# Five output projections whose two activation parts lie side by side and are read by one matmul of 512 columns

## The chip, the cores and the metric

One core of a Trainium2 chip runs the whole program as one launch. The metric is device time in microseconds, from the start to the end of one execution; lower is better. TensorE multiplies, ScalarE and VectorE convert, split and combine, GpSimd adds squares, and SyncE issues the DMAs that bring the weights.

## The reference

An activation `x` of 256 tokens by 1024 channels passes through two blocks. In the first, two layers each have a mixer (pooling with attention in layer 0, a gated recurrence in layer 1) and a convolutional feed-forward part of width 2816. The second has a mixer of four branches and a squared-ReLU feed-forward part of width 4096. Each part ends in a projection whose result is added to `x`:

```python
x = x + (concat(pool, attention) @ pa_w_out)        # 1024 -> 1024
x = x + (conv_ffn_hidden @ ffn_w_out[0])            # 2816 -> 1024
x = x + (gelu(gate) * hs) @ rg_w_out                # 1280 -> 1024
x = x + (conv_ffn_hidden @ ffn_w_out[1])            # 2816 -> 1024
x = x + gt1 * (merged @ w_o)                        # 1024 -> 1024
x = x + gt2 * (square(relu(h @ ffn_w1)) @ ffn_w2)   # 4096 -> 1024
```

RMS norms stand between the parts, so each part needs the whole of `x` from the one before it. All inputs are 32-bit floats.

## The kernel before

Everything is held transposed: 128 channels on the partitions, 256 tokens (`T`) along the free dimension. A weight matrix comes in chunks of up to eight tiles of 128x128 by SyncE's DMAs into a ring of six buffers (`ring`, `NR`). Each chunk is split in two: ScalarE rounds it to the 32-bit replicated format (`whi`, printed fp32r in the rows), and VectorE subtracts that from the chunk to get the rest (`wlo`); there are five such pairs (`NS`). The functions called `feed` do this on both engines, three to four chunks ahead of the one that TensorE uses. Activations are split in the same way, into high and low parts (`hh`/`hl`, `hidh`/`hidl`, `pah`/`pal`, `mgh`/`mgl`).

A product is then three matmuls of 256 columns for each tile of 128 input channels, all added in one PSUM bank: high weights by high activation, high weights by low activation, low weights by high activation (`linear`, L488 to L502). I call these three a tile step. Each matmul is preceded by its own weight load.

The function `residual` makes one output tile `m` of 128 channels after another (for 1024 inputs the first two together). On TensorE it calls `linear`. On VectorE it first splits the chunks up to three ahead (`feed`, L1633), then waits for output tile `m` and adds it to `x` (`add_to_x`, L1619 to L1624; for the last two projections with a multiplication by a column of `mod`), then does extra work handed in as `also`, then makes the low part of the unscaled next activation (`low_of_h`). ScalarE squares each `x` tile, GpSimd adds the squares.

Behind each projection but the last, `early` (L504 on) lets TensorE begin three output tiles of the next part with the activation that is not yet normalised, its sums of squares after the second tile step (`stats`), while VectorE and ScalarE make the normalising row (`rst`), and then the scaled activation (`raw`, then `hh` and `hl`), which the next part waits for. In the `also` slot VectorE prepares parameters of later parts (`s5p`, `w`, `tmp`, `cf` in the rows). Each engine works strictly through its own order; semaphores stand between them.

Of the kernel before, what the change touches and what calls it, by code (L numbers as in the profile page):

```python
# [7 lines left out]
F32R = mybir.dt.float32r  # L8
# [4 lines left out]
T = 256  # L13
# [207 lines left out]
def build(nc, d, out):  # L221
    with ExitStack() as ctx:
        cnt = [0]

        def alloc(stack, name, shape, dt=F32):
            cnt[0] += 1
            return stack.enter_context(nc.sbuf_tensor(f"{name}_{cnt[0]}", shape, dt))

        def signal(name):
# [32 lines left out]
        sq = alloc(st, "sq", [128, 4, T])  # L262
        vf = alloc(st, "vf", [128, 4, T])
        vt = alloc(st, "vt", [128, 2, 512])
        pah = alloc(st, "pah", [128, 8, T], F32R)
        pal = alloc(st, "pal", [128, 8, T], F32R)
        ta = alloc(st, "ta", [128, 16 + T])
        tb = alloc(st, "tb", [128, 16 + T])
        pw = alloc(st, "pw", [128, 4, 128])
# [8 lines left out]
        st.close()  # L278

        st = ExitStack()  # L280
        hidh = [alloc(st, "hidh", [128, 22, T], F32R)] * 2
        hidl = [alloc(st, "hidl", [128, 22, T], F32R)] * 2
        zu = [alloc(st, "zu", [128, 3, T])] * 2
        zg = [alloc(st, "zg", [128, 3, T])] * 2
        zl = [alloc(st, "zl", [128, 3, T])] * 2
# [14 lines left out]
        st.close()  # L300

        st = ExitStack()
        hidh[1] = alloc(st, "hidh", [128, 22, T], F32R)
        hidl[1] = alloc(st, "hidl", [128, 22, T], F32R)
        zu[1] = alloc(st, "zu", [128, 3, T])
        zg[1] = alloc(st, "zg", [128, 3, T])
        zl[1] = alloc(st, "zl", [128, 3, T])
# [25 lines left out]
        ws = alloc(s2, "ws", [128, 4, 128])  # L333
        bs_ = alloc(s2, "bs", [128, 4, 128])
        gvT = alloc(s2, "gvT", [128, 2, 256])
        mgh = alloc(s2, "mgh", [128, 8, T], F32R)
        mgl = alloc(s2, "mgl", [128, 8, T], F32R)
        bd = alloc(s2, "bd", [128, 2, 2, 64])
        cd = alloc(s2, "cd", [128, 2, 8, 16])
        cc = alloc(s2, "cc", [128, 2, 8, 16])  # L340
# [1 line left out]
        st.close()  # L342

        st = ExitStack()
        hid2h = alloc(st, "hidh2", [128, 32, T], F32R)
        hid2l = alloc(st, "hidl2", [128, 32, T], F32R)
        zz = alloc(st, "zz", [128, 4, T])
        st.close()

        MR = [mrow[:, :].rearrange("p (h t) -> p h t", h=4),  # L350
              sqt[:, 0:2, :].rearrange("p a t -> p (a t)").rearrange("p (h t) -> p h t", h=4)]

        def v4(a):
            return a[:, :, :].rearrange("p a t -> p (a t)").rearrange("p (z h t) -> p z h t", z=2, h=4)
# [82 lines left out]
        where = {}  # L437
# [23 lines left out]
        def tensor_program(e):  # L461
# [70 lines left out]
                mm(p[:, 0:T], ones, sqt[:, 2, :], False).then_inc(*stat.up(n))  # L532
                give(("stat", n), mean, n)

            def residual(n, w, nk, of, need, also=None):
                for ms in ([0, 1], [2], [3], [4], [5], [6], [7]) if nk == 8 else [[m] for m in range(8)]:
                    linear(w, ms, of, nk, need)
                    for m in ms:
                        give((w, m), resid, (n, m))
                        if also:  # L540
                            also(m)
# [32 lines left out]
            def pool_attn():  # L574
# [101 lines left out]
                    if m == 0:  # L676
                        mod_step()

                residual(1, "pa_w_out", 8, pair(pah, pal), lambda k: at_dve.wait_ge(e, ("pal", k)), also)

            def conv_ffn(l):
                w = f"ffn_w_in{l}"
                n = 2 * l + 1
                early(n)
                for i, at in enumerate(EARLY[n]):
                    give(at, ff_dve, (l, "lift", i))
                project(w, [23, 2], n)
                give((w, 23), ff_dve, (l, "g", 1))
                give((w, 2), ff_dve, (l, "u", 2))
                for m in range(2, 22):  # L690
                    if m > 2:
                        project(w, [m], n)
                        give((w, m), ff_dve, (l, "u", m))
                    project(w, [m + 22], n)
                    give((w, m + 22), ff_dve, (l, "g", m))
                    if m in ADA_IN[l]:
                        mod_step()

                def also(m):
                    mod_turn()  # L700

                residual(2 * l + 2, f"ffn_w_out{l}", 22, pair(hidh[l], hidl[l]), lambda k: ff_dve.wait_ge(e, (l, "lo", k)), also)

            def rglru():
                def ri(m):
# [57 lines left out]
            def mixers():  # L763
# [231 lines left out]
                        next(steps[at])  # L995
                for m in range(8):
                    y_of(m, 0)
                residual(5, "w_o", 8, pair(mgh, mgl), lambda k: mx_dve.wait_ge(e, ("ml", k)))

            def relu_ffn():  # L1000
                early(5)
# [13 lines left out]
            conv_ffn(1)  # L1015
            mixers()
            relu_ffn()
            residual(6, "ffn_w2", 32, pair(hid2h, hid2l), lambda k: ff_dve.wait_ge(e, (2, "lo", k)))
            stats(6)


# [524 lines left out]
        def vector_program(e):  # L1546
# [69 lines left out]
                    e.tensor_copy(shw[:, i:i + 1], ps[where[w, m]][:, T:T + 1]).then_inc(*shifted.up((n, i)))  # L1616
                return tt(o, p, rst[:, :], MUL)

            def add_to_x(n, m, p):  # L1619
                if n < 5:  # L1620
                    tt(x[:, m, :], p, x[:, m, :], ADD).then_inc(*resid.up((n, m)))
                else:
                    g = 16 if n == 5 else 40
                    stt(x[:, m, :], p, mod[:, g + m:g + m + 1], x[:, m, :], MUL, ADD).then_inc(*resid.up((n, m)))  # L1624

            def add_squares(n, m):
                square.wait_ge(e, (n, m))
# [3 lines left out]
            def residual(n, w, nk, also=None):  # L1631
                for ms in ([0, 1], [2], [3], [4], [5], [6], [7]) if nk == 8 else [[m] for m in range(8)]:
                    feed(tail(w, ms[-1], nk))  # L1633
                    for m in ms:
                        add_to_x(n, m, out_of(w, m, nk))
                        if also:
                            also(m)
                        if m and n < 6:
                            low_of_h(n, m - 1)
                if n < 6:  # L1640
                    low_of_h(n, 7)
                    feed(first(n))
# [278 lines left out]
            def rglru():  # L1921
                stat.wait_ge(e, 2)

                def taps(m):
                    src = xl[:, m, :] if m < 3 else out_of("rg_w_in", m + 10)
                    rg_act.wait_ge(e, ("x", m))
                    for s in (1, 2, 3):
                        stt(xr[:, m, s:], src[:, 0:T - s], P("rg_cw", (3 - s) * 10 + m), xr[:, m, s:], MUL, ADD).then_inc(*rg_dve.up(("x", m, s)))
                        rg_dve.wait_ge(e)
                    rg_dve.alias(("x", m))  # L1930

                def sizes(ms):
                    for m in ms:
                        rg_act.wait_ge(e, ("square", m))
                        stt(xr[:, m, :], sc[:, m % 4, :], 1.0, xr[:, m, :], ADD, MUL).then_inc(*rg_dve.up(("size", m)))

                def scan(m):
                    rg_act.wait_ge(e, ("root", m))
                    rg_pool.wait_ge(e, ("ix", m))
                    tt(ii[:, m, :], ii[:, m, :], xr[:, m, :], MUL).then_inc(*rg_dve.up(("b", m)))  # L1940
                    rg_dve.wait_ge(e)
                    rg_act.wait_ge(e, ("decay", m))
                    e.tensor_tensor_scan(xr[:, m, :], rr[:, m, :], ii[:, m, :], 0.0, MUL, ADD).then_inc(*rg_dve.up(("scan", m)))

                def times_gate(m):
                    rg_act.wait_ge(e, ("gelu", m))
                    rg_dve.wait_ge(e)
                    tt(gate[:, m, :], gate[:, m, :], xr[:, m, :], MUL).then_inc(*rg_dve.up(("y", m)))

                def low_of_y(m):  # L1950
                    rg_act.wait_ge(e, ("yh", m))
                    low_of(yl[:, m, :], gate[:, m, :], yh[:, m, :]).then_inc(*rg_dve.up(("yl", m)))

                h_tiles(2)
                for m in range(3):
                    lift(xl[:, m, :], 2, m).then_inc(*rg_dve.up(("lift", m)))
                for m in range(3):
                    taps(m)
                for m in range(3, 10):
                    feed(tail("rg_w_in", m + 10))  # L1960
                    taps(m)
                    if m in ADA_RG[0]:
                        mod_step()
                for m in range(10):
                    feed(tail("rg_w_in", m))
                    mod_turn()
                    if m in ADA_RG[1]:
                        mod_step()
                    sizes({2: (0, 1), 3: (2, 3, 4), 4: (5, 6, 7), 5: (8, 9)}.get(m, ()))
                    for i in {6: (0, 1), 7: (2,), 8: (3,), 9: (4,)}.get(m, ()):  # L1970
                        scan(i)
                    if m > 7:
                        times_gate(m - 8)
                    if m == 9:
                        low_of_y(0)
                for k in range(10):
                    if k < 5:
                        scan(k + 5)
                    if k < 8:
                        times_gate(k + 2)  # L1980
                    if k < 9:
                        low_of_y(k + 1)
                    if k == 9:
                        for m in range(8):
                            rg_pe.wait_ge(e, ("out", m))
                            add_to_x(3, m, ps[where["rg_w_out", m]][:, 0:T])
                            if m:
                                low_of_h(3, m - 1)
                        low_of_h(3, 7)
                    feed(number["rg_w_out", 0, k])  # L1990
                feed(first(3))
# [498 lines left out]
```

## Time and profile before

| | |
|---|---|
| median of 3 runs | 1174.78 us (1174.45 to 1177.47) |
| the profiled execution | 1179.18 us |
| its span, first to last instruction | 1177.4 us |
| mean granted TensorE clock | 0.975 of full |
| matmuls, and as many weight loads | 8588 |

The profile comes from one execution of its own, so sums of its rows are set against its span of 1177.4 us; 1.8 us lie around the span. L467 is the helper that issues every matmul, L1034 that of ScalarE's activations, L1551 (tensor_tensor), L1554 and L1557 those of VectorE; a row is told apart by its tile names. In matmul rows the time of one is longer than its distance to the next, since matmuls are pipelined: the distance between starts is what counts. In names such as ps<-hidh,whi the buffer number is left out, and hidh stands for the hidden activation of both feed-forward forms.

### The profile page before, as it was taken

The numbers are of one execution on the slowest core, as the hardware profiler recorded it, in microseconds if no ns is written. First come the engines' busy times: TensorE is split into PE (matmuls) and PEld (weight loads), VectorE is DVE, ScalarE is ACT, GpSimd is POOL, SyncE is SP. The second block draws the span as 40 slices with busy tenths as digits, with TensorE's granted clock in tenths as the row PEclk, the third lists the DMA queues.
The fourth block names the chain that finished last, engine by engine and source line by source line (L and its number), as shares of the span: only waits on it lengthen the run. The fifth ranks groups of instructions, "written<-read, shape, count | busy, mean of one in ns | idle before, by whom it ended". The sixth has DMA issues, their size and how long they took to land.

```text
span 1177.4 us, 21014 instructions
## 1 busy us (share of the span) xinstructions
PE 1093.6 (93%) x8588; PEld 1039.9 (88%) x8588; DVE 837.4 (71%) x1444; ACT 641.6 (54%) x1098; POOL 67.5 (6%) x79
## 2 busy tenths in 40 slices
PE   6997999999979788999999989899999979999996
PEld 6875999999978688899999978799989979999996
DVE  6464998888894486887787778898875576655443
ACT  6544676665645965655555585322233457875441
POOL 2131100000002001000001000000000011000010
PEclk9998999999999988999999989999999989999999
DMA  9267465555555573565675642222324274656641
GB/s 335 70 210 280 154 186 191 180 166 194 160 195 173 213 252 106 179 237 194 249 252 179 206 143 69 81 88 92 106 97 155 80 252 132 201 184 191 196 143 36
DMA packets 59856, 200.41 MB, mean 170 GB/s; under 512 B 6768, under 2 KB 11504, under 8 KB 59632
## 3 DMA queue, kind: packets, MB, share of 16 engines
q1 hardware_dynamic: 58032, 194.54, 49.9%
q10 hardware_dynamic: 1728, 4.53, 1.1%
q8 instruction: 68, 1.11, 0.4%
q14 instruction: 28, 0.23, 0.1%
HBM read 197.99 MB, written 1.05 MB: 169 GB/s over the span
## 4 chain that ended last, share of the span: by engine, by line
PE 75%; DVE 14%; ACT 6%; DMA 2%; issue 1%; SPq 0%; ACTq 0%; DVEq 0%
PE ps L467 75%; DVE wlo L1551 4%; ACT whi L1034 2%; DVE rst L1580 1%; ACT L1034 1%; DVE raw L1551 1%; DMA ring<-ffn_w_out 1%; DVE raw L1557 1%; DMA ring<-pa_w_in 1%; DVE hl L1557 1%; DVE hl L1551 1%; ACT rr L1034 0%; DVE x L1551 0%; ACT xr L1034 0%; ACT raw L1034 0%
## 5 line engine op out<-in xcount | busy, mean ns | idle before, releaser
L467 PE MATMUL ps<-hh,whi 128*128 128x256 f32 (+1 forms) x1656 | 484.1, 292 | 40.3 <-DVE wlo L1551 38.4
L467 PE MATMUL ps<-hh,wlo 128*128 128x256 f32 (+1 forms) x1656 | 473.7, 286 | 0.0
L467 PE MATMUL ps<-hl,whi 128*128 128x256 f32 (+1 forms) x1656 | 472.1, 285 | 0.0
L1551 DVE TENSOR_TENSOR wlo<-ring,whi 128x1024 fp32r<-128x1024 f32 (+1 forms) x313 | 376.4, 1217 | 66.7 <-ACT whi L1034 65.8
L1034 ACT ACTIVATE whi<-ring 128x1024 fp32r<-128x1024 f32 (+1 forms) x313 | 323.0, 1040 | 102.6 <-PE ps L467 62.1
L467 PEld LDWEIGHTS ps<-hh,whi 128*128 128x128 f32 x1656 | 319.1, 193 | 61.8 <-issue 32.9
L467 PEld LDWEIGHTS ps<-hl,whi 128*128 128x128 f32 x1656 | 319.8, 193 | 1.4 <-issue 1.0
L467 PEld LDWEIGHTS ps<-hh,wlo 128*128 128x128 f32 x1656 | 319.4, 193 | 0.0
L467 PE MATMUL ps<-hidh,whi 128*128 128x256 f32 x608 | 172.3, 283 | 2.3 <-DVE wlo L1551 2.3
L467 PE MATMUL ps<-hidl,whi 128*128 128x256 f32 x608 | 172.0, 283 | 0.0
L467 PE MATMUL ps<-hidh,wlo 128*128 128x256 f32 x608 | 172.0, 283 | 0.0
L467 PEld LDWEIGHTS ps<-hidh,whi 128*128 128x128 f32 x608 | 116.7, 192 | 3.4 <-DVE wlo L1551 1.8
L467 PEld LDWEIGHTS ps<-hidl,whi 128*128 128x128 f32 x608 | 116.7, 192 | 0.0
L467 PEld LDWEIGHTS ps<-hidh,wlo 128*128 128x128 f32 x608 | 116.7, 192 | 0.0
L2330 POOL TENSOR_TENSOR sqa<-sqa,sqt 128x256 f32<-128x256 f32 x36 | 34.2, 951 | 963.9 <-ACT sqt L1034 963.9
L1557 DVE SCALAR_TENSOR_TENSOR zg<-ps,vec,zg 128x255 f32<-128x255 f32 x84 | 40.4, 481 | 24.8 <-ACT zg L1034 23.2
L1034 ACT ACTIVATE sqt<-x 128x256 f32<-128x256 f32 x49 | 20.1, 414 | 65.7 <-DVE x L1551 34.1
L1557 DVE SCALAR_TENSOR_TENSOR zu<-ps,vec,zu 128x255 f32<-128x255 f32 x80 | 38.5, 481 | 17.0 <-ACT zu L1034 14.5
L1034 ACT ACTIVATE zg<-ps,vec 128x256 f32<-128x256 f32 x42 | 23.6, 562 | 47.1 <-PE ps L467 47.1
L1034 ACT ACT_TABLE_LOAD x35 | 44.9, 1283 | 6.4 <-issue 4.2
L1034 ACT ACTIVATE zu<-ps,vec 128x256 f32<-128x256 f32 x40 | 22.5, 563 | 29.8 <-PE ps L467 23.6
L467 PE MATMUL ps<-yin,ring 128*128 128x256 f32 x160 | 38.6, 379 | 0.0
(360 smaller groups left out, 1348.9 us busy)
## 6 DMA issues: line engine op xcount, KB each, us to landing
ring<-ffn_w_in SPq DMA_DIRECT2D x88, 512.0 KB, 4.3
ring<-ffn_w SPq DMA_DIRECT2D x64, 512.0 KB, 4.4
ring<-w_in SPq DMA_DIRECT2D x51, 512.0 KB, 3.6
ring<-ada_w SPq DMA_DIRECT2D x48, 512.0 KB, 5.2
ring<-ffn_w_out SPq DMA_DIRECT2D x32, 448.0 KB, 4.5
ring<-rg_w_in SPq DMA_DIRECT2D x20, 512.0 KB, 4.3
ring<-pa_w_in SPq DMA_DIRECT2D x16, 512.0 KB, 6.6
ring<-ffn_w_out SPq DMA_DIRECT2D x16, 512.0 KB, 3.7
```

What stands on the lines that cost most here:

```text
L467: return e.matmul(o, l, r, start=start, stop=stop)
L1034: return e.activation(o, i, func, bias=bias, scale=scale, accum_out=acc)
L1551: return e.tensor_tensor(o, a, b, op)
L1557: return e.scalar_tensor_tensor(out=o, in0=a, scalar=s, in1=b, op0=op0, op1=op1)
L1580: e.reciprocal(rst[:, :], rst[:, :]).then_inc(*mean.up(("rst", n)))
L2330: e.tensor_tensor(sqa[:, :], sqa[:, :], sqt[:, m % 2, :], ADD).then_inc(*sum_g.up((n, m)))
```

## The change

The high and low part of an activation get one array in which tile k's 256 high columns are followed by its 256 low columns. In five of the six projections (all but rg_w_out) one matmul of 512 columns reads both against the high weights and fills a whole bank: columns 0 to 255 hold high by high, columns 256 to 511 high by low. The matmul with the low weights still has 256 columns and adds to the first half. VectorE adds both halves to `x`, one after the other, and the second waits for the first. The arrays take the same room as before. Cut to its core:

```diff
-        pah = alloc(st, "pah", [128, 8, T], F32R)
-        pal = alloc(st, "pal", [128, 8, T], F32R)
+        pa2 = alloc(st, "pa2", [128, 8, 2, T], F32R)
...
+        (pah, pal), (mgh, mgl), (hid2h, hid2l) = ((a[:, :, 0, :], a[:, :, 1, :]) for a in (pa2, mg2, hid2))
+        hidh, hidl = ([a[:, :, v, :] for a in hid] for v in range(2))
...
+            def wide(w, ms, both, nk, need):
+                outs = [take((w, m)) for m in ms]
+                for parts in zip(*(chunks(w, m, nk) for m in ms)):
+                    k, n = parts[0][1:]
+                    for q in range(n):
+                        need(k + q)
+                        for (c, _, _), o in zip(parts, outs):
+                            low.wait_ge(e, c)
+                            j = turn[c] % NS
+                            last = k + q == nk - 1
+                            if last:
+                                mm(o[:, 0:T], wlo[j][:, q, :], both[:, k + q, 0, :], False, False)
+                            t = mm(o[:, :], whi[j][:, q, :], both[:, k + q, :, :], k + q == 0, last)
+                            if not last:
+                                t = mm(o[:, 0:T], wlo[j][:, q, :], both[:, k + q, 0, :], False, False)
+                            if q == n - 1:
+                                t.then_inc(*through.up(c))
...
-            def residual(n, w, nk, of, need, also=None):
+            def residual(n, w, nk, both, need, also=None):
                 for ms in ([0, 1], [2], [3], [4], [5], [6], [7]) if nk == 8 else [[m] for m in range(8)]:
-                    linear(w, ms, of, nk, need)
+                    wide(w, ms, both, nk, need)
...
-            def add_to_x(n, m, p):
-                if n < 5:
-                    tt(x[:, m, :], p, x[:, m, :], ADD).then_inc(*resid.up((n, m)))
-                else:
-                    g = 16 if n == 5 else 40
-                    stt(x[:, m, :], p, mod[:, g + m:g + m + 1], x[:, m, :], MUL, ADD).then_inc(*resid.up((n, m)))
+            def add_to_x(n, m, parts):
+                for i, p in enumerate(parts):
+                    if i:
+                        resid.wait_ge(e)
+                    if n < 5:
+                        t = tt(x[:, m, :], p, x[:, m, :], ADD)
+                    else:
+                        g = 16 if n == 5 else 40
+                        t = stt(x[:, m, :], p, mod[:, g + m:g + m + 1], x[:, m, :], MUL, ADD)
+                    t.then_inc(*resid.up((n, m) if p is parts[-1] else (n, m, i)))
...
-                        add_to_x(n, m, out_of(w, m, nk))
+                        p = out_of(w, m, nk)
+                        add_to_x(n, m, (p, ps[where[w, m]][:, T:2 * T]))
```

## Rows read from the trace of the kernel before

**Rows 1.** The page: busy time of the engines, share of the span, instructions.
```profile
PE 1093.6 (93%) x8588; PEld 1039.9 (88%) x8588; DVE 837.4 (71%) x1444; ACT 641.6 (54%) x1098; POOL 67.5 (6%) x79
```

**Rows 2.** The page: chain that ended last, shares of the span by engine.
```profile
PE 75%; DVE 14%; ACT 6%; DMA 2%; issue 1%; SPq 0%; ACTq 0%; DVEq 0%
```

**Rows 3.** Timeline in ffn_w2: start us, length us, engine, operation, tiles.
```profile
1163.05 0.28 PE L467 MATMUL ps<-hidl,whi 128*128 128x256 f32 x1
1163.05 0.19 PEld L467 LDWEIGHTS ps<-hidh,wlo 128*128 128x128 f32 x1
...
1166.05 0.28 PE L467 MATMUL ps<-hidh,wlo 128*128 128x256 f32 x1
```

**Rows 4.** Timeline of TensorE: matmuls of 258 columns behind w_o.
```profile
985.02 0.28 PE L467 MATMUL ps<-hh,whi 128*128 128x258 f32 x1
...
987.41 0.28 PE L467 MATMUL ps<-hh,wlo 128*128 128x258 f32 x1
```

**Rows 5.** Timeline of TensorE in pa_w_out, behind an idle stretch.
```profile
111.38 1.12 PE L570 MATMUL ps<-cst,mrow 128*128 128x128 f32 x4 [2.53 <-ACT mrow L1034]
...
112.94 0.41 PE L467 MATMUL ps<-pah,whi 128*128 128x256 f32 x1
...
114.22 0.41 PE L467 MATMUL ps<-pah,whi 128*128 128x256 f32 x1
```

**Rows 6.** Timeline of TensorE: matmuls in plain 32-bit, merged.
```profile
47.42 1.84 PE L467 MATMUL ps<-cst,sq 128*128 128x2 f32 x16
...
939.81 5.56 PE L467 MATMUL ps<-yin,ring 128*128 128x256 f32 x25
```

**Rows 7.** Chain of waits through pa_w_out and ffn_w_out0: start us, us, what.
```profile
116.42 0.42 DVE x L1551
...
131.80 0.35 DVE x L1551
...
142.31 157.45 PE ps L467 x1311
...
308.05 1.15 DVE wlo L1551
...
309.24 5.67 PE ps L467 x45
...
318.88 0.34 DVE x L1551
...
325.87 0.33 DVE x L1551
...
336.66 1.15 DVE wlo L1551
```

**Rows 8.** Chain of waits through ffn_w_out1.
```profile
602.28 8.15 PE ps L467 x66
...
610.87 55.45 PE ps L467 x462
...
666.34 0.42 DVE x L1551
```

**Rows 9.** Chain of waits through w_o.
```profile
953.28 27.95 PE ps L467 x211
...
981.26 0.44 DVE rst L1554
```

**Rows 10.** Chain of waits through ffn_w2 to the end.
```profile
1009.91 156.80 PE ps L467 x1308
...
1166.73 0.49 DVE x L1557
```

**Rows 11.** Timeline of VectorE around w_o, idle time before in brackets.
```profile
940.66 0.42 DVE L1551 TENSOR_TENSOR cosT<-ps,cosT 128x256 f32<-128x256 f32 x1 [1.81 <-PE ps L467]
941.12 0.42 DVE L1551 TENSOR_TENSOR cosT<-cosT,pm 128x256 f32<-128x256 f32 x1
...
978.22 0.48 DVE L1557 SCALAR_TENSOR_TENSOR x<-ps,mod,x 128x256 f32<-128x256 f32 x1 [0.70 <-PE ps L467]
...
979.99 1.22 DVE L1551 TENSOR_TENSOR wlo<-ring,whi 128x1024 fp32r<-128x1024 f32 x1
```

**Rows 12.** Windows: stretch, its us, VectorE busy us, clock, DMA share, GB/s.
```profile
602.00:666.00 64.00, 51.04 (x84) 1.00 0.63 208
```

More of the change, by code:

```diff
@@ L280, in build @@
         st = ExitStack()
-        hidh = [alloc(st, "hidh", [128, 22, T], F32R)] * 2
-        hidl = [alloc(st, "hidl", [128, 22, T], F32R)] * 2
+        hid = [alloc(st, "hid", [128, 22, 2, T], F32R)] * 2
         zu = [alloc(st, "zu", [128, 3, T])] * 2
@@ L302, in build @@
         st = ExitStack()
-        hidh[1] = alloc(st, "hidh", [128, 22, T], F32R)
-        hidl[1] = alloc(st, "hidl", [128, 22, T], F32R)
+        hid[1] = alloc(st, "hid", [128, 22, 2, T], F32R)
         zu[1] = alloc(st, "zu", [128, 3, T])
@@ L335, in build @@
         gvT = alloc(s2, "gvT", [128, 2, 256])
-        mgh = alloc(s2, "mgh", [128, 8, T], F32R)
-        mgl = alloc(s2, "mgl", [128, 8, T], F32R)
+        mg2 = alloc(s2, "mg2", [128, 8, 2, T], F32R)
         bd = alloc(s2, "bd", [128, 2, 2, 64])
@@ L344, in build @@
         st = ExitStack()
-        hid2h = alloc(st, "hidh2", [128, 32, T], F32R)
-        hid2l = alloc(st, "hidl2", [128, 32, T], F32R)
+        hid2 = alloc(st, "hid2", [128, 32, 2, T], F32R)
         zz = alloc(st, "zz", [128, 4, T])
@@ L677, in also @@
                         mod_step()
-                residual(1, "pa_w_out", 8, pair(pah, pal), lambda k: at_dve.wait_ge(e, ("pal", k)), also)
+                residual(1, "pa_w_out", 8, pa2, lambda k: at_dve.wait_ge(e, ("pal", k)), also)
             def conv_ffn(l):
@@ L700, in also @@
                     mod_turn()
-                residual(2 * l + 2, f"ffn_w_out{l}", 22, pair(hidh[l], hidl[l]), lambda k: ff_dve.wait_ge(e, (l, "lo", k)), also)
+                residual(2 * l + 2, f"ffn_w_out{l}", 22, hid[l], lambda k: ff_dve.wait_ge(e, (l, "lo", k)), also)
             def rglru():
@@ L997, in mixers @@
                     y_of(m, 0)
-                residual(5, "w_o", 8, pair(mgh, mgl), lambda k: mx_dve.wait_ge(e, ("ml", k)))
+                residual(5, "w_o", 8, mg2, lambda k: mx_dve.wait_ge(e, ("ml", k)))
             def relu_ffn():
@@ L1017, in tensor_program @@
             relu_ffn()
-            residual(6, "ffn_w2", 32, pair(hid2h, hid2l), lambda k: ff_dve.wait_ge(e, (2, "lo", k)))
+            residual(6, "ffn_w2", 32, hid2, lambda k: ff_dve.wait_ge(e, (2, "lo", k)))
             stats(6)
@@ L1985, in rglru @@
                             rg_pe.wait_ge(e, ("out", m))
-                            add_to_x(3, m, ps[where["rg_w_out", m]][:, 0:T])
+                            add_to_x(3, m, (ps[where["rg_w_out", m]][:, 0:T],))
                             if m:
```

## The prediction

> **What bounds the kernel now.** I read the page first: TensorE is busy 93% of the span and VectorE 71% [rows 1], and the chain that ended last is 75% TensorE and 14% VectorE [rows 2]. So a faster tile step on TensorE pays, but only where TensorE is on that chain, and 40 more VectorE operations cost wherever VectorE is. I therefore read the timeline for what one matmul takes from start to start, and then the chain of waits through each of the five projections.
>
> The slot. In ffn_w2 25 slots lie between the starts at 1163.05 and 1166.05 us, so one is 0.120 us, and the load of the next weights starts together with the matmul before it [rows 3]. A tile step is three slots, 0.360 us. What fills a slot decides everything, since the columns streamed stay the same: 3 x 256 before, 512 + 256 after. Three observations. At half clock six slots take 1.28 us, 0.2133 each [rows 5], which is 256 columns at 1.2 GHz and nothing on top; at 2.4 GHz the same stream needs 0.107. Matmuls of 258 columns have 20 slots in 2.39 us, 0.1195 each [rows 4]: two columns more, no longer slot. And 16 matmuls that stream only two columns still need (1.84 - 0.25)/15 = 0.106 us each, if the last lasts 0.25 [rows 6]. So the 0.120 is not the stream. It is the weight load, which starts when the previous matmul starts and must be over before the next; a stream of 256 columns at full clock is just too short to cover it. A stream twice as long does cover it: the plain 32-bit matmuls on `yin` have slots of (5.56 - 0.38)/24 = 0.216 us [rows 6], the 0.213 of 512 columns with 0.003 on top, though each has its own weight load.
>
> **The change, part by part.**
>
> *The tile step.* Removed: one matmul and one weight load in 8 x (8 + 22 + 22 + 8 + 32) = 736 tile steps. The 512-column matmul should take the `yin` slot, 0.216 us, and hide the load of `wlo` in it; the 256-column one leaves too little cover for the next load, as today, and takes 0.120. Together 0.336 against 0.360: 24 ns gained per tile step. No row has this alternation, so both bounds: at best the pair takes its bare stream, 768 columns at 2.4 GHz, 0.320 (40 ns gained); at worst the wide matmul takes two of today's slots (nothing gained). I take 24, nearest to the two rows that it is made of. At half clock the pair takes what the three take, so tile steps there gain nothing.
>
> A rule of the Trainium skill speaks against the change. What the trace shows is a slot of 0.120 us [rows 3]. "TensorE: Matmul & The Clock Gate", section "Back-to-back issue gap", gives a matmul of N columns N/2.4 + 2.5 ns, and its section on LDWEIGHTS gives 128 columns 107 ns, less than that. An estimate from this page: 109 ns for 256 columns, 216 ns for 512, so 3 x 109 = 327 becomes 325, and 2 to 3 ns are gained. The trace does not agree about the slot before (120, not 109); about 512 columns of stream it does (0.216 [rows 6]).
>
> *The second addition.* It must wait for the first. A dependent pair on VectorE starts 941.12 - 940.66 = 0.46 us apart [rows 11]; I take 0.46 for each of the 24 additions in the first three projections. For those of w_o and ffn_w2, which last 0.48 to 0.49 instead of 0.42 [rows 10, 11], I take 0.52. A bound from below is 0.34, the share of an addition on the chain when the next operation does not depend on it [rows 7].
>
> Now the five projections, each by what its chain says.
>
> *pa_w_out.* From 116.42 to 142.31 the chain runs through VectorE nearly all the way: its splits, the parameter work and the additions of tiles 2 to 7, of which the first is at 116.42 and the last at 131.80 [rows 7]. TensorE is ahead of it, and what it saves buys nothing here. Six additions on the chain give 6 x 0.46 = 2.76. Ahead of 116.42 the additions of tiles 0 and 1 hold up ScalarE's `mrow` copy, which TensorE waits for before 111.38 [rows 5]: 0.46, less some 0.3 from about 12 tile steps at full clock ahead of 116.42. Sum +2.9. The three `early` tiles wait for their `wlo` behind these additions, so TensorE, done sooner, will stand there, some 3 us longer than now. After 2.53 us of idling it ran at half clock [rows 5]; if it does here, VectorE is still later than it, and I price that at 0 to 1 us and leave it in the range.
>
> *ffn_w_out0.* TensorE has the chain up to 142.31 + 157.45 = 299.76, through tiles 0 to 4: 110 tile steps, -2.64. Then VectorE, with its block of `cf` parameters, is late until the `wlo` at 308.05; TensorE stands until 309.24 [rows 7]. The second addition of tile 4 stands ahead of that block: +0.46. Then 45 matmuls of TensorE, 15 tile steps, -0.36; then VectorE again with additions 6 and 7 and on to the split at 336.66 that the next part waits for, +0.92 [rows 7]. Sum -1.6: of 176 tile steps 125 count.
>
> *ffn_w_out1.* TensorE has all 66 + 462 matmuls on the chain [rows 8], 176 tile steps, -4.22. VectorE is busy 51.0 of 64 us [rows 12]; an output tile takes 7.92 us now and 7.39 then, VectorE's share of it is 51.0/8 = 6.4 and becomes 6.9, so it stays hidden on the mean. The last addition leads into the normalising chain: +0.46. Sum -3.8. DMA brings 208 GB/s here at a share of 0.63 [rows 12]; 7% more is still far from full.
>
> *w_o.* The wait in front is for the merged tiles, which are untouched. Of the 211 matmuls on the chain 22 are those of `early` and `stats`, which leaves 63 tile steps; 27.95 - 211 x 0.120 = 2.6 us is the excess of steps at half clock (0.28 each), at most nine, fewer since the plain 32-bit matmuls of `stats` are in it. I take seven, so 56 count [rows 9]: -1.34. At its end `rst` starts at 981.26, straight after the split that began at 979.99 and lasted 1.22, and that one follows addition 7 at 978.22 on VectorE [rows 9, 11]: the second addition is passed on, +0.52. Sum -0.8.
>
> *ffn_w2.* 256 tile steps on the chain, -6.14; the last addition at 1166.73 is followed by the closing norm [rows 10], +0.52. Sum -5.6.
>
> Gains: 125 + 176 + 56 + 256 = 613 tile steps x 0.024 = 14.7 us. Costs: 2.9 + 1.38 + 0.46 + 0.52 + 0.52 = 5.8 us. Net -8.9, so the span goes from 1177.4 to 1168.5. The profiled execution, at 1179.18, lay 4.4 us above the median of the runs; the same difference from the median of 1174.78 gives 1165.9, so 1166.
>
> The other additions (tiles 0 to 6 of ffn_w2 and w_o, most of the two ffn_w_out) cost nothing, because VectorE waits there for TensorE; were that cover gone, those 27 would cost 12 us. `feed`, the DMAs and the queues keep their order. The new internal wait of `add_to_x` holds up `also`, `low_of_h` and the next split behind it, and through them TensorE, which is what the terms above price.
>
> **Rivals.**
>
> 1. The pair is better than 0.336: the load hides under the wide matmul and is partly done before the narrow one starts, 0.328 or the bare stream 0.320. Then 613 x 0.032 = 19.6 or 24.5 are gained; in ffn_w_out1 VectorE begins to bind (an output tile down to 7.0 to 7.2 us), 0.5 to 1.5 back. Net -13.3 or -17: 1161 or 1158. For it: the load alone took 0.106 [rows 6]. Against: between two matmuls of 256 columns the slot is 0.120 all the same.
>
> 2. The 13 ns above the bare stream (0.120 against 0.107) belong to each matmul and not to the load. The pair is then 0.320 + 2 x 0.013 = 0.347, 13 ns gained: -8.0 + 5.8 = -2.2, 1172.6, no change that shows. Against: half clock shows none of the 13 [rows 5], `yin` only 3 [rows 6].
>
> 3. Slower: VectorE's second addition in pa_w_out and at the four other ends costs its 5.8 us whatever TensorE gains. It decides from a gain below 5.8/613 = 9.4 ns per tile step, that is, a pair above 0.351. By the mechanism that slots follow the stream alone with a small fixed part, the gain is 2.5 ns: 613 x 0.0025 = 1.5, net +4.3, 1179. With no gain at all it is +5.8, 1181. Against: 258 columns are not longer than 256 [rows 4]. The skill's page named above would have it this way.
>
> 4. The tile step gains its 24 ns, but a longer stand of TensorE behind pa_w_out brings half clock, or shifted waits in the mixers cost a few us: 1169 to 1171.
>
> Measured differences under 0.3% (3.5 us) can't be told from none.
>
> **Chances and range.** Forecast 0.55; rival 1 0.16; rival 2, with pairs of 0.344 (-4.0, 1170.8) counted to it, 0.14; rival 3 0.07; rival 4 0.08. The range of 1160 to 1173 holds the forecast, rival 4, rival 2 and the milder half of rival 1; it leaves out rival 3 and the bare stream, some 0.15. Faster by over 0.3% means below 1171.3: forecast, rival 1, rival 4 and a small part of rival 2, 0.79. Within 0.3%: 0.14. Slower: 0.07.
>
> **What would show it.** In ffn_w2 of the changed kernel the wide slot should be 0.216 us, the narrow one 0.120, the pair 0.336; ffn_w2 should shrink from 256 x 0.360 = 92.2 to 86.0 us. In pa_w_out the chain should still be VectorE's, with the additions in twos 0.46 apart, and the next part's start at 142.31 should come 2.9 us later. The stand before ffn_w_out0's tile 6 should grow by about 1.0 us (TensorE saves six tiles' worth, 3.2, and the `wlo` comes 2.2 earlier). At the end there should be two operations on `x` in front of the last squares. The prediction is wrong if the pair is at 0.347 or above, if it is at 0.328 or below, or if VectorE falls behind in ffn_w_out1.

## The result and the profile after

| | before | after |
|---|---|---|
| median of 16 runs | 1174.98 us (1174.20 to 1179.69) | 1179.26 us (1174.62 to 1182.18) |
| profiled execution, its span | 1179.18, 1177.4 us | 1179.61, 1177.8 us |
| mean granted clock | 0.975 | 0.970 |
| matmuls | 8588 | 7852 |

The ratio is 1.0027, 95% interval 1.0015 to 1.0039: 3.2 us slower, 1.8 to 4.6. (It compares the means of the runs; the medians lie 4.3 us apart.) The forecast was 8.9 us faster with a range of 1160 to 1173. The two profiled executions differ by only 0.4 us, so the stages are compared below by distances inside each trace and the whole by the ratio.

The page after, engines and the matmuls of the two wide kinds (lines of rows 1, and what became of the three `hidh`/`hidl` groups):

```profile
PE 1092.1 (93%) x7852; PEld 1002.7 (85%) x7852; DVE 854.6 (73%) x1484; ACT 641.8 (54%) x1098; POOL 67.8 (6%) x79
...
L466 PE MATMUL ps<-hid,whi 128*128 128x512 f32 x608 | 213.9, 399 | 2.4 <-DVE wlo L1570 2.4
L466 PE MATMUL ps<-hid,wlo 128*128 128x256 f32 x608 | 166.8, 281 | 0.0
```

736 matmuls are gone, but TensorE is busy 1092.1 instead of 1093.6 us [rows 1], and VectorE has 17 us more. The timeline of TensorE in ffn_w2 after the change, to be read against rows 3:

```profile
1110.27 0.39 PE L466 MATMUL ps<-hid,whi 128*128 128x512 f32 x1
1110.50 0.28 PE L466 MATMUL ps<-hid,wlo 128*128 128x256 f32 x1
1110.62 0.40 PE L466 MATMUL ps<-hid,whi 128*128 128x512 f32 x1
1110.85 0.28 PE L466 MATMUL ps<-hid,wlo 128*128 128x256 f32 x1
1110.97 0.40 PE L466 MATMUL ps<-hid,whi 128*128 128x512 f32 x1
1111.21 0.28 PE L466 MATMUL ps<-hid,wlo 128*128 128x256 f32 x1
1111.33 0.40 PE L466 MATMUL ps<-hid,whi 128*128 128x512 f32 x1
...
1112.39 0.40 PE L466 MATMUL ps<-hid,whi 128*128 128x512 f32 x1
```

Six pairs take 1112.39 - 1110.27 = 2.12 us, 0.353 each: a wide slot of about 0.236 and a narrow one of 0.117. Forecast were 0.216 and 0.120. A tile step gained 7 ns, not 24. From its first matmul to its last, ffn_w2 took 90.2 us (1076.0 to 1166.2) where it had taken 92.0 (1074.4 to 1166.4): 1.8 less, not 6.1.

VectorE in pa_w_out, timeline after (the additions of tiles 2, 3, 6 and 7):

```profile
117.62 0.88 DVE L1570 TENSOR_TENSOR x<-ps,x 128x256 f32<-128x256 f32 x2 [2.33 <-PE ps L466]
...
121.28 0.87 DVE L1570 TENSOR_TENSOR x<-ps,x 128x256 f32<-128x256 f32 x2
...
131.64 0.87 DVE L1570 TENSOR_TENSOR x<-ps,x 128x256 f32<-128x256 f32 x2
...
134.78 0.87 DVE L1570 TENSOR_TENSOR x<-ps,x 128x256 f32<-128x256 f32 x2
```

There is no idle time in brackets from the second pair to the last: VectorE goes from addition to addition without waiting, as forecast. The last begins at 134.78 where it began at 131.80 [rows 7]. The chain of waits after goes on:

```profile
133.18 1.68 DVE wlo L1570
...
134.91 3.89 PE ps L466 x16
...
138.82 0.44 DVE rst L1573
...
146.58 151.78 PE ps L466 x1173
```

The next part starts at 146.58 instead of 142.31, 4.3 us later; 2.9 was forecast. The chain is not VectorE's all the way: 16 matmuls of TensorE, 3.89 us, stand in it, which were not in it before. The end of the program, chain after:

```profile
1166.62 0.49 DVE x L1576
...
1167.14 0.49 DVE x L1576
```

The second addition stands there with 0.52 us, as forecast.

### The profile page after: what moved, and what is told of

Its sections match the earlier page's. It is cut to its first block, busy times and chain, and to the rows that moved or that the text cites. A ratio compares the mean times of both kernels' runs of the same rounds, so it can differ in the third digit from the quotient of the medians.

```text
span 1177.8 us, 19582 instructions
## 1 busy us (share of the span) xinstructions
PE 1092.1 (93%) x7852; PEld 1002.7 (85%) x7852; DVE 854.6 (73%) x1484; ACT 641.8 (54%) x1098; POOL 67.8 (6%) x79
## 4 chain that ended last, share of the span: by engine, by line
PE 74%; DVE 15%; ACT 7%; DMA 2%; issue 1%; ACTq 0%; SPq 0%; DVEq 0%
PE ps L466 73%; DVE wlo L1570 4%; ACT whi L1053 1%; ACT L1053 1%; DVE rst L1599 1%; DVE x L1570 1%; DVE raw L1570 1%; DVE raw L1576 1%; DVE hl L1570 1%; DVE xr L1576 1%; DMA ring<-pa_w_in 1%; DVE hl L1576 1%; ACT rr L1053 0%; DMA ring<-rg_w_out 0%; ACT hh L1053 0%
## 5 line engine op out<-in xcount | busy, mean ns | idle before, releaser
L466 PE MATMUL ps<-hid,whi 128*128 128x512 f32 x608 | 213.9, 399 | 2.4 <-DVE wlo L1570 2.4
L466 PE MATMUL ps<-hid,wlo 128*128 128x256 f32 x608 | 166.8, 281 | 0.0
L466 PEld LDWEIGHTS ps<-hid,whi 128*128 128x128 f32 x608 | 113.0, 188 | 29.6 <-DVE wlo L1570 2.7
L466 PEld LDWEIGHTS ps<-hid,wlo 128*128 128x128 f32 x608 | 114.8, 189 | 2.1
L1053 ACT ACTIVATE sqt<-x 128x256 f32<-128x256 f32 x49 | 20.2, 416 | 78.8 <-DVE x L1570 44.5
L1576 DVE SCALAR_TENSOR_TENSOR x<-ps,mod,x 128x256 f32<-128x256 f32 x32 | 15.4, 484 | 34.8 <-PE ps L466 34.2
L1570 DVE TENSOR_TENSOR hid<-zz,hid 128x256 fp32r<-128x256 f32 x32 | 13.5, 425 | 35.0 <-ACT hid L1053 35.0
```

The source lines that it names most:

```text
L466: return e.matmul(o, l, r, start=start, stop=stop)
L1053: return e.activation(o, i, func, bias=bias, scale=scale, accum_out=acc)
L1570: return e.tensor_tensor(o, a, b, op)
L1576: return e.scalar_tensor_tensor(out=o, in0=a, scalar=s, in1=b, op0=op0, op1=op1)
```

## The experiments

A ratio is against the kernel before on the same chip; times in microseconds.

| kernel | ratio (95%) | against before |
|---|---|---|
| changed kernel | 1.0027 (1.0015 to 1.0039) | +3.2 |
| e1: VectorE's part alone | 1.0050 (1.0032 to 1.0069) | +5.9 |
| e2: TensorE's part alone | 0.9960 (0.9941 to 0.9979) | -4.7 |
| e3: pa_w_out as before | 0.9988 (0.9972 to 1.0004) | -1.4 |
| e4: runs of one width | 1.0006 (0.9993 to 1.0019) | +0.7 |
| e5: e4, pa_w_out as before | 0.9983 (0.9969 to 0.9996) | -2.0 |
| e6: e5, old way where VectorE is on the chain | 0.9965 (0.9952 to 0.9979) | -4.1 |
| e7: pa_w_out alone changed | 1.0056 (1.0036 to 1.0076) | +6.6 |
| e8: changed kernel, stand filled | 1.0017 (0.9999 to 1.0035) | +2.0 |

**What a slot holds (m1).** A kernel of its own: streams of one width on TensorE, 64 matmuls or more with a weight load each, in the rounded format (r), in plain 32-bit and in bf16 (b), with nothing else running and then beside VectorE (V), ScalarE (A) and DMAs (D). It computes none of the reference.

```diff
+    ("r", (512,), 64, ""), ("r", (384,), 64, ""), ("r", (320,), 64, ""),
...
+    ("b", (512,), 64, ""),
...
+    ("r", (512,), 96, "V"), ("r", (256,), 160, "V"), ("r", (512,), 96, "A"), ("r", (256,), 160, "A"),
+    ("r", (512,), 96, "D"), ("r", (256,), 160, "D"), ("r", (512,), 96, "VAD"), ("r", (256,), 160, "VAD"),
```

> Matmuls alone, streams of equal slots with no other engine at work, then the same beside VectorE, ScalarE and DMAs. The kernel computes none of the reference; it only multiplies real data and hands out sums of it. Theory S (the rounded format streams slower than a column per cycle at 2.4 GHz): alone, 512 columns take about 0.233 us, 384 about 0.175, 256 about 0.118, in proportion down to where the weight load binds near 0.112. Theory W (a fixed piece of some 20 ns of the weight load is left uncovered): 512 takes 0.233, 384 0.180, 320 0.153, that is 0.107 per 256 columns plus a constant. Theory C (others' traffic to the memories slows the stream): alone 512 takes 0.216 and 256 0.112, and the 0.233 shows only beside VectorE, ScalarE or DMA. My prediction's reading (load bound at 256, bare stream at 512) is the first half of theory C.

Timeline of TensorE, each answer cut to one width, merged (start, length, tiles, form, count):

```profile
36.73 12.63 PE L110 MATMUL ps<-mr,wr 128*128 128x512 f32 x55
...
50.82 9.36 PE L110 MATMUL ps<-mr,wr 128*128 128x384 f32 x53
...
61.80 8.38 PE L110 MATMUL ps<-mr,wr 128*128 128x320 f32 x56
...
70.72 7.00 PE L110 MATMUL ps<-mr,wr 128*128 128x256 f32 x57
...
86.83 5.41 PE L110 MATMUL ps<-mr,wr 128*128 128x128 f32 x47
...
190.27 2.10 PE L110 MATMUL ps<-mb,wb 128*128 128x512 bf16 x9
```

A slot is the length without the last matmul's own (0.39, 0.33, 0.31, 0.28, 0.28 and 0.38 us) over the count less one: 0.2267 for 512 columns, 0.1737 for 384, 0.1467 for 320, 0.120 for 256, 0.112 for 128; in bf16 0.215 for 512. From 256 columns up that is N/2.4 plus 13 ns: 213.3 + 13.4, 160 + 13.7, 133.3 + 13.4, 106.7 + 13.3. Only at 192 and 128 columns does something else bind, at 0.112 in both, whatever the width; I take it for the weight load. So theory W has it, as to the form: a fixed 13 ns for every matmul in the rounded format from 256 columns up (what it belongs to, this run does not say), 2 ns in bf16. Plain 32-bit matmuls of 256 columns, with nothing beside them, took 0.216 as in the kernel before. Theory C falls: beside VectorE, ScalarE, DMA or all three, slots of equal width were 0.227 and 0.120 again. S falls, since 512 would have to be two times 0.120.

**Why the pair is worse than the sum of its slots (m2).** By the slots of m1 a pair should take 0.2267 + 0.120 = 0.347, yet the changed kernel has 0.353. m1 also had two stretches of pairs: alone, behind 64 columns, a pair took 0.347; behind 256 columns and beside VectorE, ScalarE and DMAs together, 0.353. The same kernel with pairs:

```diff
+    ("r", (256,), 160, ""), ("r", (512, 256), 128, ""), ("r", (512,), 48, ""), ("r", (512, 256), 128, ""),
+    ("r", (384,), 48, ""), ("r", (512, 256), 128, ""), ("b", (512,), 48, ""), ("r", (512, 256), 128, ""),
+    ("r", (320,), 48, "V"), ("r", (512, 256), 128, "V"), ("r", (320,), 48, "A"), ("r", (512, 256), 128, "A"),
...
+    ("r", (320,), 48, ""), ("r", (512,) * 8 + (256,) * 8, 128, ""),
...
+    ("b", (512,), 48, ""), ("b", (512, 256), 96, ""),
```

> Matmuls in the rounded format alone again, now alternating 512 and 256 columns behind four different lead-ins, then beside VectorE, ScalarE or DMAs one at a time, then in runs of eight wide and eight narrow ones. It computes none of the reference. Known from the runs of equal widths: a slot is N/2.4 plus 13.3 ns from 256 columns up. Theory F (a fixed part alone): every pair takes 0.347 us. Theory R (alternation has a rhythm of its own, set by the lead-in and not by load): some pairs keep to 0.347 and others to 0.353, with and without load, and runs of eight take (8 x 0.227 + 8 x 0.120)/8 = 0.347 always. Theory L (load brings the 0.353): all unloaded phases 0.347, the loaded ones 0.353.

Timeline of TensorE, one row for each stretch of pairs (behind 256 columns; behind 384; behind bf16; beside VectorE; beside ScalarE; the last in bf16):

```profile
39.83 12.42 PE L107 MATMUL ps<-mr,wr 128*128 128x512 f32 x69
...
103.76 14.49 PE L107 MATMUL ps<-mr,wr 128*128 128x256 f32 x83
...
135.75 14.61 PE L107 MATMUL ps<-mr,wr 128*128 128x512 f32 x83
...
165.74 14.52 PE L107 MATMUL ps<-mr,wr 128*128 128x512 f32 x81
...
195.74 14.54 PE L107 MATMUL ps<-mr,wr 128*128 128x512 f32 x81
...
315.81 9.48 PE L107 MATMUL ps<-mb,wb 128*128 128x512 bf16 x57
```

Pairs: (12.42 - 0.39)/34 = 0.354; (14.49 - 0.28)/41 = 0.347; (14.61 - 0.39)/41 = 0.347; (14.52 - 0.39)/40 = 0.353 beside either engine; in bf16 (9.48 - 0.38)/28 = 0.325. The same code alternates in two rhythms. One keeps to 0.347; the other to 0.353, and unloaded stretches show either, so the slower one needs no load. The changed kernel's ffn_w2 is in the second: the pairs shown above take 0.35, 0.35 and 0.36 in turn, 0.353 on the mean. Runs of eight wide and eight narrow ones took 0.2301 + 0.1190 = 0.349 per pair. Theory R holds, but for the runs, which are 2 ns above it. What chooses the rhythm stays open. Unloaded pairs took 0.347 behind 64 or 384 columns and behind bf16, and 0.353 behind 256 and 512; all four loaded stretches took 0.353, three of them behind 320 columns, and no unloaded one stood behind 320, so a share of the load in the choice is not excluded. Two further alternations, unloaded: 512 and 384 columns took 0.413 a pair, 13 ns above the sum of their slots, and 384 and 256 took 0.293, exactly the sum.

**VectorE's part alone (e1).** Three matmuls of 256 columns, the low product in the second half:

```diff
-                            t = mm(o[:, :], whi[j][:, q, :], both[:, k + q, :, :], k + q == 0, last)
+                            mm(o[:, 0:T], whi[j][:, q, :], both[:, k + q, 0, :], k + q == 0, False)
+                            t = mm(o[:, T:2 * T], whi[j][:, q, :], both[:, k + q, 1, :], False, last)
```

> The five projections keep three matmuls of 256 columns per tile step, but high weights by low activation goes into the second half of the bank, and VectorE adds both halves in two dependent operations. So only VectorE's part of the change is in it. Theory A (VectorE's second additions cost 5.8 us on the chain, TensorE's gain in the changed kernel is about 6 ns per tile step, 613 x 0.006 = 3.7): this runs 5.8 us above the kernel before, near 1181, ratio 1.005. Theory B (the cost is smaller, 2 us or less, and the changed kernel's loss comes from elsewhere, as from its wide matmuls or the clock): below 1177.5.

+5.9 us, 3.8 to 8.1. The forecast's sum for the additions, 5.8, stands as a sum; its shares were otherwise, as ffn_w_out0 shows below.

**TensorE's part alone (e2).** The second half of the bank is not added; the product of high weights and low activation is missing from the sum.

```diff
-                        add_to_x(n, m, (p, ps[where[w, m]][:, T:2 * T]))
+                        add_to_x(n, m, (p,))
```

> The changed kernel with its 512-column matmuls, but VectorE adds only the first half; the product of high weights and low activation is left out of the sum. So only TensorE's part of the change is in it. Theory A: 613 tile steps x 6 to 7 ns = 4 us below the kernel before, near 1171, and 5.8 to 8 us below the changed kernel. Theory B: within 1.5 us of the kernel before or above it. By the predicted 24 ns it would have been 14.7 us below, at 1160.

-4.7 us, 2.5 to 6.9: at 613 tile steps on the chain 7.7 ns each, in line with the 6.7 of the trace and far from the 24 forecast. The two parts together give +1.2, each uncertain by 2.2.

**pa_w_out as before (e3), and alone (e7, with the condition reversed).** The additions follow the same condition.

```diff
-                    wide(w, ms, both, nk, need)
+                    if w == "pa_w_out":
+                        linear(w, ms, lambda k: (both[:, k, 0, :], both[:, k, 1, :]), nk, need)
+                    else:
+                        wide(w, ms, both, nk, need)
```

> The changed kernel with pa_w_out as before (three matmuls of 256 columns, one addition). Theory A (six additions of 0.46 us on VectorE's chain there and a longer stand of TensorE with half clock behind it): it takes back 3 to 4 us of the loss, to 1175.5 to 1176.5, and ffn_w_out0 begins at 260 instead of 264 us. Theory B (the loss sits elsewhere): no more than 1 us, 1178 or above.

> Only pa_w_out is changed (wide matmuls, two additions), the other four projections as before. Theory A (the additions on VectorE's chain there and the longer stand of TensorE behind them are the whole loss of this projection): ffn_w_out0 begins 3 to 4.5 us later than in the kernel before and the whole is that much slower, 1178 to 1180, ratio 1.0025 to 1.004. Theory B (the delay is made good later, since the next part waits for other things): within 1 us of the kernel before.

Taking it out of the change gives back 3.2 + 1.4 = 4.6 us; alone it costs 6.6 (4.2 to 8.9), more than the 3 to 4.5 expected. From the first matmul of pa_w_out to the first of ffn_w_out0 the traces have 159.6 us before (100.4 to 260.0), 164.2 after, 163.5 in e1, 160.3 in e3 and 165.5 in e7. The other runs give the spread of such a distance, one profile each: 158.0 to 160.3 with one addition in pa_w_out (before, e3, e5, e6), 162.3 to 165.5 with two (after, e1, e4, e7, e8). So one of the two smallest projections costs about as much as TensorE gains in the whole program, and it does so on VectorE and through the clock; that the rest would be faster without it is not shown, since e3's interval reaches 1.0004. Windows behind it, in the kernel before, after and e7 in this order:

```profile
131.00:136.00 5.00, 4.64 (x36) 4.32 (x35) 3.96 (x7) 2.28 (x5) 0.00 (x0) 1.00 0.50 162
136.00:141.00 5.00, 5.00 (x44) 5.00 (x43) 4.96 (x11) 2.10 (x5) 0.00 (x0) 1.00 0.24 91
```

```profile
131.00:136.00 5.00, 2.51 (x15) 2.20 (x15) 4.90 (x10) 3.49 (x7) 0.74 (x1) 0.85 0.38 112
136.00:141.00 5.00, 5.00 (x33) 4.90 (x33) 3.29 (x5) 1.86 (x4) 0.00 (x0) 0.81 0.56 204
```

```profile
131.00:136.00 5.00, 2.44 (x15) 1.84 (x13) 4.93 (x9) 4.27 (x7) 1.48 (x2) 0.92 0.50 174
136.00:141.00 5.00, 4.97 (x19) 4.62 (x20) 3.05 (x6) 1.76 (x3) 0.00 (x0) 0.50 0.47 153
```

The columns are the stretch, its length, busy time of TensorE's matmuls, its weight loads, VectorE, ScalarE, GpSimd, then the granted clock. Between 131 and 136 TensorE is busy 2.5 of 5 us where it was busy 4.6, since it waits for the third early `wlo`; and then the clock is 0.81 or 0.50, where it was 1.00.

**The stand filled (e8).** Ten matmuls whose sums go nowhere ahead of the second and of the third early tile:

```diff
+                        if n == 1 and k == 0 and i:
+                            for v in range(10):
+                                mm(fill[:, 0:T], whi[j][:, 0, :], hh[:, 0, 0:T], v == 0, v == 9)
```

> The changed kernel, with 20 extra matmuls of 256 columns (2.4 us at full clock, their sums go nowhere) in the stand of TensorE behind pa_w_out, ten ahead of the second and ten ahead of the third early tile. They ask for nothing that isn't there. If the half clock behind that stand is part of the loss, it disappears there (granted clock 1.00 between 131 and 142 us instead of about 0.85) and ffn_w_out0 begins 0.5 to 1.5 us earlier than 264 us; if VectorE alone sets that start, it stays at 264 within 0.3.

```profile
131.00:136.00 5.00, 5.00 (x38) 4.65 (x36) 4.90 (x10) 4.77 (x8) 1.76 (x2) 1.00 0.57 199
136.00:141.00 5.00, 4.54 (x34) 4.34 (x34) 3.93 (x8) 2.18 (x4) 0.00 (x0) 1.00 0.37 120
```

The clock is 1.00 throughout, and the distance to ffn_w_out0 is 163.9 instead of 164.2. Taken alone that would be the second of the two answers. But this profile had lost time ahead of the filling: from the first matmul of pa_w_out to the one that reads `mrow` it took 12.6 us, the changed kernel 11.3. Behind the stand the two timelines of TensorE part, the changed kernel first, then e8:

```profile
134.91 0.58 PE L466 MATMUL ps<-hh,whi 128*128 128x256 f32 x1 [2.49 <-DVE wlo L1570]
...
137.64 0.72 PE L466 MATMUL ps<-sqa,cst 128*128 128x256 f32 x2
```

```profile
136.55 0.39 PE L466 MATMUL ps<-hh,whi 128*128 128x256 f32 x1 [0.46 <-DVE wlo L1576]
...
138.10 0.60 PE L466 MATMUL ps<-sqa,cst 128*128 128x256 f32 x2
```

The twelve matmuls ahead of the sums of squares take 2.73 us in the changed kernel and 1.55 in e8. VectorE's `rst` needs these sums: in the changed kernel it waits for them, in e8 TensorE is no longer on the chain there. From the addition of tile 6 to the start of the next part are 13.6 us before, 14.9 after and 14.1 in e8. So the half clock behind the stand is part of the loss, some 0.7 us in this profile; by the same measure 0.5 in e1, 0.6 in e4 and 1.5 in e7. The whole runs at 1.0017; the interval contains both the changed kernel's ratio and 1.

**Runs of one width (e4, e5), and the old way where it counts (e6).** In e4 a chunk's wide matmuls come first and its narrow ones behind them (a last chunk the other way round):

```diff
+                    elif not last:
+                        high()
+                        rest()
```

> The changed kernel, but the matmuls of a chunk are put in runs: all with 512 columns together, all with 256 together, so that a width hardly ever follows the other. Same matmuls, same additions. If the alternation costs 6 ns per tile step (0.353 against 0.347), ffn_w2 shrinks from 90.5 to 88.9 us and the whole by 613 x 0.0064 = 3.9 us, to about 1175. If the alternation isn't the cause: no change from 1179.

> The runs of one width, and pa_w_out as before with one addition. If both parts add up: 3.9 and 4 to 4.6 us below the changed kernel, 1171, ratio to the kernel before 0.9965. If VectorE's lateness elsewhere eats TensorE's gain: 1173 to 1175.

> As the kernel with runs and the old pa_w_out, and in the other four projections the last output tile, and in ffn_w_out0 also tiles 4 and 6, in the old way with a single addition: these are the additions that my sum put on the chain of waits (1.38 + 0.46 + 0.52 + 0.52 = 2.9 us); their 162 tile steps give up 13 ns each, of which some 106 were on the chain, 1.4 us. So 1.5 us below the kernel with runs and the old pa_w_out, about 1169.5. If these additions were hidden after all, it is 1.4 us above it.

The timeline of e4 in ffn_w2, three runs:

```profile
1089.72 2.00 PE L466 MATMUL ps<-hid,whi 128*128 128x512 f32 x8
1091.56 2.08 PE L466 MATMUL ps<-hid,wlo 128*128 128x256 f32 x16
1093.47 2.91 PE L466 MATMUL ps<-hid,whi 128*128 128x512 f32 x12
```

Wide slots are (2.00 - 0.39)/7 = 0.230, narrow ones (2.08 - 0.28)/15 = 0.120. ffn_w2 took 89.0 us instead of the changed kernel's 90.2. e4 is 2.5 us below the changed kernel by the ratios, with intervals that overlap a little; 0.349 instead of 0.353 on 613 tile steps gives 2.5, and my 3.9 took 0.347. e5 takes off another 2.7, less than the 4 to 4.6 that e3 had suggested, within both intervals. e6 comes to 0.9965, 4.1 us faster than the kernel before, which is clear of noise, and 2.1 below e5, where 1.5 was expected and the intervals overlap; it is the fastest version here that computes the whole sum. Each of its rules comes from one term of the sum. In the traces its rule for ffn_w_out0 shows: from the first matmul there to the next part's first behind the norm are 78.8 us in e5 and 78.0 in e6.

## Why the prediction was wrong

**The step that failed** is "The 512-column matmul should take the `yin` slot, 0.216 us". It took 0.236. The price was borrowed from plain 32-bit matmuls, which have 3 ns above their stream; in the rounded format every matmul from 256 columns up has 13 ns above it (m1), and alternating the two widths cost a further 6 to 7 ns per pair (m2, the slower rhythm). The reading behind it, that today's 0.120 is the weight load and that a longer stream covers it, failed too: the floor that I take for the load is 0.112, and what a slot has above its stream at 256 columns it has at 512 as well (m1). My three observations did not carry it. At half clock the 13 ns are absent, but they are an effect of full clock alone; 258 columns showed 0.1195 on the mean, but single slots there lie between 0.11 and 0.13, too far apart for a difference of 0.8 ns; and the two-column matmuls gave the floor of the load, which is below 0.120 and so argued against me. Their 0.106 was misread as well: the first slot of that row lasts 0.03 us and the other fourteen 0.112 each.

Rival 2 described the slot rightly, a fixed 13 ns per matmul and a pair of 0.347, and the rhythm carried it on to 0.353. That lies past rival 3's point of decision, 0.351: with 6.7 ns the 613 tile steps gain 4.1 us against 5.8, which is +1.7.

**The sum.** VectorE's 5.8: 5.9 measured (e1). TensorE's 14.7: 4.7 measured (e2). *pa_w_out*, +2.9: 4.6 in the profile, from its first matmul to the first behind the norm (46.5 us against 41.9). Four additions, those of tiles 2 to 5, follow each other without a wait and cost 14.09 - 12.32 = 1.8 us where 1.84 were priced. Behind the addition of tile 6 it is 1.3 instead of 0.9, of which the half clock there takes some 0.7, which I had left to the range (0 to 1). Ahead of the addition of tile 2 it is 1.5, where I had 0.15. Windows there, before and after, and behind them the row of the changed kernel that answers to the first of rows 5:

```profile
109.00:118.00 9.00, 6.62 (x43) 6.62 (x44) 7.02 (x19) 5.59 (x9) 1.35 (x2) 0.81 0.91 329
```

```profile
109.00:118.00 9.00, 6.60 (x23) 5.76 (x24) 6.34 (x15) 4.50 (x7) 0.76 (x1) 0.62 0.89 331
```

```profile
111.40 1.12 PE L589 MATMUL ps<-cst,mrow 128*128 128x128 f32 x4 [3.00 <-ACT mrow L1053]
```

The clock in this stretch was 0.62 instead of 0.81, behind TensorE's wait for `mrow`, which grew from 2.53 [rows 5] to 3.00 us. I had priced the wait and not the clock. It is not so in every execution: from the first matmul on `mrow` to the addition of tile 2 are 5.0 us before and 6.2 after; e7 has 6.2 too, at a clock of 0.63 in this stretch, but e1, e4 and e8, with the same additions, have 4.9 to 5.1 at 0.81.

*w_o*: a similar matter, -0.8 forecast. The chain after has this:

```profile
954.26 25.21 PE ps L466 x126
...
979.50 0.50 DVE x L1576
...
980.02 0.49 DVE x L1576
...
983.01 0.35 DVE rst L1573
```

From TensorE's piece to `rst` are 28.8 us, and 28.0 were before [rows 9]. The two additions, 0.52 apart, are on it now, as forecast. TensorE gave less than the 24 ns a tile step, and the clock between 949 and 963 us was 0.63 where it had been 0.76. In e3 and e8, with the same code there and a clock of 0.76 in the like stretch, it is 27.3 and 27.2 us: the forecast -0.8 came out in them, though not by its terms.

*ffn_w_out0*, -1.6 forecast. Chain after:

```profile
315.41 0.34 DVE x L1570
...
331.02 0.35 DVE x L1570
...
342.26 2.27 DVE wlo L1570 x2
```

From the first matmul of ffn_w_out0 (264.3, before 260.0) to the `wlo` that the next part waits for are 78.0 us, and 76.7 were before [rows 7]: +1.3. It is 78.0 in e3 and e8 too, 78.7 in e1 and 76.0 in e2, so it is no accident of one profile. 125 tile steps at 6.7 ns and the 1.38 for additions would give +0.5. The rest is a stretch of chain that I had given to TensorE: before, its 45 matmuls from 309.24 on led to tile 6 [rows 7]; now VectorE, behind its `cf` block, goes through three splits to the addition of tile 5, at 315.41, and on. TensorE's 15 tile steps buy nothing there and one more addition counts. The stand of TensorE ahead of 313.46 grew from 1.57 to 2.40 us, near the 1.0 forecast, but by luck: TensorE came 0.9 us earlier, not 3.2, and the `wlo` 0.1 earlier, not 2.2.

*ffn_w_out1*, -3.8 forecast: from its first matmul to the reciprocal that makes `rst` 71.3 us before, 70.8 after, 70.2 in e3 and 70.0 in e8. TensorE's own stretch became 1.4 us shorter, but the chain leaves it:

```profile
612.52 41.56 PE ps L466 x236
...
666.98 0.35 DVE x L1570
```

From 654.08 to the last addition it runs through ScalarE's and VectorE's splits and parameter work, and that addition follows three splits without a pause, where VectorE had waited 0.84 us for TensorE before. So VectorE did fall behind at the last tile, one of the signs of being wrong, and at a TensorE far slower than forecast; it is little, since TensorE's last matmul had ended only some 0.2 us earlier.

*ffn_w2* kept its form: TensorE's chain with the smaller gain, the closing 0.52 as forecast.

**The rule of the Trainium skill.** "TensorE: Matmul & The Clock Gate", section "Back-to-back issue gap", gives N/2.4 + 2.5 ns, and m1 and m2 agree with it in bf16: 0.215 to 0.216 at 512 columns, 0.325 for a pair of 512 and 256. In the rounded format it is 11 ns short per matmul. I had given its outcome, 1179, a chance inside 0.07. The time came out near there, though by another road: a gain of 6.7 ns, and a dearer pa_w_out and ffn_w_out0, instead of a gain of 2.5.

**What stays open.** With 6.7 ns for the pair the sum is +1.7, and e1 and e2 add up to +1.2. The 0.8 of ffn_w_out0 and some 0.7 for the half clock behind pa_w_out bring it to 3.2, and the lower clock ahead of tile 2 to 4.4 in profiles that have it; measured are 3.2, 1.8 to 4.6. That it closes is an account of single profiles and not shown by the ratios, whose intervals are as wide as these terms. The origin of the 13 ns at full clock, and of the two rhythms, was not found.

## What to carry to other kernels

Price a matmul's slot only from rows of its own number format: the same stream of columns has 2 to 3 ns above it in bf16 or plain 32-bit and 13 ns in the rounded 32-bit format here. Merging two matmuls saves that fixed part once, and a second operation on the engine that drains the bank can cost more than it: multiply both by the counts on the chain of waits, not by the counts in the program. Where the two alternate, put equal widths in runs, and leave the old form at the few tiles whose drain is on the chain; here that turned 1.0027 into 0.9965, though the last of these steps alone is not clear of noise. Follow the chain again once an engine has got work: here it left TensorE in two projections that the forecast had counted as TensorE's.

## What was not expected of the hardware

- A fixed 13.3 ns per matmul in the rounded 32-bit format at full clock (0.2267, 0.1737, 0.1467 and 0.120 us at 512, 384, 320 and 256 columns), absent at half clock (0.2133 at 256, [rows 5]).
- Two rhythms of a strict alternation of 512 and 256 columns, 0.347 and 0.353 us a pair, in one kernel without any load; 512 and 384 columns are 13 ns above the sum of their slots, 384 and 256 not.
- No effect of VectorE, ScalarE or DMAs (226 GB/s beside 512 columns, 166 beside 256) on slots of equal width: 0.227 and 0.120 us.
